# Larger packets for a decoder trunk's cache copies and near rows

## The reference

```
h = rms_norm(x, norm_g)
proj = einsum('btd,de->bte', h, w_in)
... convolution group -> ya, pooling group -> yb
kk = concatenate([k_buf, k], axis=1)
vv = concatenate([v_buf, v], axis=1)
o = dilated_attention(q, kk, vv, k_buf.shape[1])     # dilations 1, 4, 16, keys by stride
yc = o.reshape(B, T, C_ATT) * silu(c_gate)
new_k, new_v = kk[:, -2048:], vv[:, -2048:]
y = einsum('bte,ed->btd', concatenate([ya, yb, yc]), w_out);  return x + y, ...
```

## Time and profile before

| what | us |
|---|---|
| median of 3 runs | 404.59 |
| lowest, highest | 402.63, 405.35 |
| the profiled execution | 401.57 |
| its span, first to last instruction | 399.7 |

### The profile page before, as it was taken

The page is one execution under the profiler, slowest core; times in us unless marked ns, Lnnn a source line. Parts: engine busy times, 40 slices in busy tenths (PEclk is TensorE's granted clock), DMA queues, the critical chain, the costliest instruction groups (busy, mean ns, idle before and its releaser), DMA issues.

```text
span 399.7 us, 4745 instructions
## 1 busy us (share of the span) xinstructions
PE 347.5 (87%) x1550; PEld 273.4 (68%) x1550; DVE 232.6 (58%) x530; ACT 100.2 (25%) x237; POOL 58.8 (15%) x110
## 2 busy tenths in 40 slices
PE   3898799999889859899948999999979877989990
PEld 2686578887667636588827888888757654758870
DVE  2604669859977976620103489978984997541010
ACT  4200012542523123500111011453352222320011
POOL 4006830000600002044000420000600011000000
PEclk9999969999889899999986999999979988989997
DMA  8999999999999999999999999999999999999983
GB/s 293 412 419 412 418 418 417 418 407 411 417 419 408 418 392 406 396 418 418 416 398 387 414 418 416 417 411 420 418 419 417 414 357 361 372 374 372 396 347 118
DMA packets 44329, 157.73 MB, mean 395 GB/s; under 512 B 6988, under 2 KB 20116, under 8 KB 44306
## 3 DMA queue, kind: packets, MB, share of 16 engines
q0 software_dynamic: 14624, 88.25, 54.6%
q10 hardware_dynamic: 14420, 41.52, 26.3%
q1 hardware_dynamic: 15262, 27.67, 18.7%
HBM read 140.23 MB, written 104.46 MB: 612 GB/s over the span
## 4 chain that ended last, share of the span: by engine, by line
PE 43%; DVE 13%; SPq 12%; ACTq 11%; DMA 10%; issue 5%; ACT 4%; DVEq 0%
PE pj L693 23%; SPq L479 11%; DMA kg<-in_cache_k_win 10%; PE pj L836 8%; ACTq L459 4%; DVE yc L1296 3%; ACTq L465 3%; PE psc L765 3%; PE ptr L611 3%; DVE ssc L1240 2%; ACTq L463 2%; PE ps L813 1%; ACTq L874 1%; DVE spsum_pad L1266 1%; DVE tok L1234 1%
## 5 line engine op out<-in xcount | busy, mean ns | idle before, releaser
L693 PE MATMUL pj<-hT,wt 128*128 128x264 f32 x800 | 197.9, 407 | 6.3 <-DVE hT L1151 4.5
L693 PEld LDWEIGHTS pj<-hT,wt 128*128 128x128 f32 x800 | 159.0, 202 | 39.7 <-issue 11.6
L1296 DVE SCALAR_TENSOR_TENSOR yc<-u_ext,par,yc 128x256 f32<-128x256 f32 x180 | 77.2, 481 | 3.8 <-DVE u_smp L1180 1.0
L836 PE MATMUL pj<-mix,wt 128*128 128x264 f32 x256 | 61.2, 395 | 0.0
L836 PEld LDWEIGHTS pj<-mix,wt 128*128 128x128 f32 x256 | 49.1, 194 | 8.5
L600 POOL DMA_DIRECT2D out<-in_cache_v_win x48 | 26.2, 554 | 142.3 <-issue 142.3
L1366 DVE TENSOR_TENSOR xT<-xT,pj 128x264 f32<-128x264 f32 x16 | 6.9, 430 | 55.9 <-PE pj L836 55.9
L600 POOL DMA_DIRECT2D out<-in_cache_k_win x48 | 26.5, 561 | 83.6 <-issue 83.6
L954 ACT ACTIVATE ex<-pj 128x264 f32<-128x264 f32 x22 | 8.6, 391 | 78.3 <-PE pj L693 45.2
L1178 DVE SCALAR_TENSOR_TENSOR u_ext<-ex,pj 128x256 f32<-128x256 f32 x6 | 2.5, 422 | 30.5 <-ACT ex L954 30.5
L1234 DVE TENSOR_TENSOR tok<-kg,qb 128x1536 f32<-128x1536 f32 x10 | 17.6, 1758 | 3.4 <-DMA kg<-in_cache_k_win 3.0
(11 more groups left out here) (187 smaller groups left out, 339.6 us busy)
## 6 DMA issues: line engine op xcount, KB each, us to landing
wt<-in_w_tiles ACTq DMA_DIRECT2D x62, 512.0 KB, 33.2
out<-in_cache_k_win POOLq DMA_DIRECT2D x24, 1080.0 KB, 44.4
out<-in_cache_v_win POOLq DMA_DIRECT2D x24, 1080.0 KB, 81.1
out<-in_cache_k_win POOLq DMA_DIRECT2D x8, 1200.0 KB, 72.7
out<-in_cache_v_win POOLq DMA_DIRECT2D x8, 1200.0 KB, 87.9
out<-in_cache_k_win POOLq DMA_DIRECT2D x16, 432.0 KB, 65.1
out<-in_cache_v_win POOLq DMA_DIRECT2D x16, 432.0 KB, 86.2
kg<-in_cache_k_win SPq DMA_DIRECT2D x32, 144.0 KB, 36.0
```

Of the source, the lines that this page charges most:

```text
L693: last = nc.tensor.matmul(pj[n % RING][:, 0:T], wt[:, g % WRING, k, :], hT[:, k, :], start=(k == 0), stop=(k == KD - 1))
L836: last = nc.tensor.matmul(pj[n % RING][:, 0:T], wt[:, g % WRING, k, :], mix[:, k, :], start=(k == 0), stop=(k == KD - 1))
L1296: last = V.scalar_tensor_tensor(out=yc[:, t, 0:SEQ], in0=x_w, scalar=par[:, ROW_CW + w * CT + t:ROW_CW + w * CT + t + 1], in1=yc[:, t, 0:S ...
```

## The change

Only the lengths of the pieces change; the transfers, their order and their bytes stay. `NEAR_BYTES` goes from 4 rows (6144 B) to 8 (12288 B), so that a partition's near rows are one packet in gathers and stores. `DEEP_BYTES`, for layer 1's copies, goes from a third of 15 rows (7680 B) to half of them (11520 B). Layer 0's copies, cut into pieces of 5 rows (7680 B), are cut into 5 pieces for each of 16 parts: 9 rows (13824 B) for the copy of 720 rows and 10 rows (15360 B) for that of 800.

```diff
-COPY_BYTES = PIECE_ROWS * C_ATT * 4
-DEEP_BYTES = (DEEP_STEP - 1) * C_ATT * 4 // 3
+PIECES = 5
+DEEP_BYTES = (DEEP_STEP - 1) * C_ATT * 4 // 2
 BLOCK_BYTES = (FAR_STEP - 1) * C_ATT * 4
...
-NEAR_BYTES = 4 * C_ATT * 4
+NEAR_BYTES = GATHER[0][2] * C_ATT * 4
...
                     else:
-                        dst, src = (t.rearrange("(c e r) h d -> c e (r h d)", c=16, r=PIECE_ROWS) for t in (out[l, s, a:b], cache[l, s, a + 1:b + 1]))
-                        size = COPY_BYTES
+                        dst, src = (t.rearrange("(c e r) h d -> c e (r h d)", c=16, e=PIECES) for t in (out[l, s, a:b], cache[l, s, a + 1:b + 1]))
+                        size = (b - a) // (16 * PIECES) * C_ATT * 4
```

## The result

The changed kernel takes 450.62 us (median of 4 runs, 448.08 to 459.79), the kernel before it, timed beside it, 404.97 us (402.63 to 409.78): a ratio of 1.1113, with a 95% interval of 1.1068 to 1.1158. The run of 459.79 was a slow one and is left out of the ratio. Slower, as forecast, but by 46 us where 26 to 31 were forecast, and outside the range of 412 to 446.

A forecast was written before the change was run, and what follows sets the result against it. It took the full DMA engines, served in turns by packet, to bound the kernel through late gathers and ACT's held issue. Span 399.7 + 34 - 1 = 433, 434.6 us per execution, lowered to 431; range 412 to 446.

The forecast's parts named there:

- F: ACT's issue before layer 1, held by its full queue: +26 us, so PE starts layer 1 at 237 us.
- A: Landing of layer 0's first gathered keys: +6.3 us, so DVE starts at 94.7 us.
- D: Landing of layer 1's gathered keys: +34.7 us, at 305.6; DVE waits 8 us and everything after is late by 34.
- Turns: At the DMA engines: one packet of each busy queue in turn, whatever the sizes; a turn lasts 0.417 us.
- B: Landing of layer 0's first gathered values: +12.3 us, at 161.1 us; PE is +10.2 us from here.
- The size of a turn: q0's mean turn grows 67 ns in layer 1's copies, 112 in layer 0's: turns of 0.48 and 0.53 us.
- a gain of 4864 x 9.5 ns/16 = 2.9 us: Over all transfers: 4864 fewer packets, each saving a fixed 9.5 ns, take 2.9 us off DMA time.
- The weights have slack too: Weight tiles for PE: claimed to have time to spare and add no wait; no size given.
- E: Landing of layer 1's gathered values: +25 us, at 358, before PE's 369; no new wait; last copy near 350.
- The end: Compute after layer 1's keys are read, 128.2 us with idle DMA: about 1 us back, span 433 us.
- weights bind as well: Rival: during layer 0's copies a weight tile takes 4.8 us where PE needs about 4; 447 us, chance 10%.

The follow-up runs named there:

- small_copies: The kernel before with copies in packets of 4608 B (4800 B in transfers of 800 rows), near rows still 6144 B: 410.61 us, ratio 1.0255.
- after_no_value_stores: The changed kernel without layer 0's stores of gathered value rows, which ACT issues into q10: 435.46 us, ratio 1.0881 to the kernel before.
- after_no_key_stores: The changed kernel without layer 0's stores of gathered key rows, which SP issues into q1: 442.87 us, ratio 1.1061 to the kernel before.
- no_copies: The kernel before without all of POOL's cache copies and the waits for them: 378.8 us, ratio 0.9466.
- half_copies: The kernel before with copies of 7680 B set to 3840 B, near rows and far blocks unchanged: 402.8 us, ratio 0.9974.

## Why the prediction was wrong in size

The order of the forecast held (larger packets of q0, longer turns, late gathers, a later end). Two steps failed: the lengthening of a turn was put too low, +67 ns where it was +97, and the hold of ACT at its issues was counted only at F, although ACT's tile issues also delay the compute before A and add 16.6 us between F and D. By its own steps:

- **Turns** ("an engine serves them in turns, one packet of each, whatever the sizes"): right. Counts were equal at every size that was run, and small_copies shows the opposite sign at A, B and D. The Trainium skill's rule ("DMA: Bandwidth & Descriptors", section "Queues, rings and completion order"), a round-robin at packet granularity, agrees with 594, 596 and 596. Equal counts show that no queue gets ahead, not that the engines change queue after every single packet.
- **The size of a turn** ("The others' turn of 0.417 us becomes 0.48 and 0.53"): this term was mis-sized. From the counts of 100 to 200 us, a turn was 1600/3896 = 0.411 us and is 1600/3147 = 0.508: +97 ns where +67 were forecast. q0's own part went from 0.584 x 0.411 = 0.240 to 0.632 x 0.508 = 0.321, +81 for 1904 B more, where the fit's 0.0380 ns per byte gives +72; most of the rest is q10's, whose packets took 0.131 us instead of 0.122. In 200 to 300 us a turn is 0.555. The step behind it, a fit of 26.3 B/ns and 9.5 ns a packet taken as fixed, fell: all engines together moved 396 GB/s where it had been 411. That this is the memory, where q0 counts double, is argued above and not shown. For the same reason "a gain of 4864 x 9.5 ns/16 = 2.9 us" was not there, at least in the copies (277.03 against 276.42 us alone).
- **A**: right within 1.6 us (96.3 for 94.7), by luck in good part. q0 had 2536/16 = 158 turns by then, where the forecast counted 180 less some 8 for its 2 us of dry time; POOL waited 33.3 us for its state load, where it had waited 26.7, and in 40 to 46 us q0 had 71 packets beside 355 of q10. So q0 fell dry as assumed, but for longer, and that made up for turns that were longer than forecast. DVE's wait was 2.0 us instead of 9, because DVE itself was 9 us late, with no gather in its way: ACT's issue of five tiles took 13.23 us from 23.11 on (7.66 before), and three more in 62 to 74 us took 2.4 to 2.9 each instead of 0.3. In the chain of the first 100 us ACT's issuing of tiles has 22.7%.
- **B**: 170.0 for 161.1. From A to B it took 142.5 turns before, (5282 - 3002)/16, and (4818 - 2536)/16 = 142.6 after, so no turn was saved by the merged near rows; each took 0.517 instead of 0.425 us, 13 us in all where +6 were forecast.
- **F**: the mechanism was right (ACT's issue, not the data, decides), the size again the turn's: 248.7 for 237.
- **D**: "DVE would come at 271.5 + 26 = 297.5 and waits 8 us" (the compute keeps its pace behind F, and the keys decide) is the step that failed by mechanism, and "The weights have slack too" hid it. The weight tiles did land in time, some 20 us ahead of use by a rough reading of landings against readers, and I had looked at landings alone. But ACT, which issues them between its own computations, is held at each issue while its queue is behind. ACT's tile issues in layer 1 before the change,

```profile
268.87 0.34 ACTq L874 DMA_DIRECT2D wt<-in_w_tiles  x1
...
277.71 0.33 ACTq L874 DMA_DIRECT2D wt<-in_w_tiles  x1
...
282.16 0.33 ACTq L874 DMA_DIRECT2D wt<-in_w_tiles  x1
```

and after it (the row at 303.85 is one of the computations between the issues, for which PE waits):

```profile
288.60 3.37 ACTq L874 DMA_DIRECT2D wt<-in_w_tiles  x1
...
292.88 4.45 ACTq L874 DMA_DIRECT2D wt<-in_w_tiles  x1
...
298.25 4.28 ACTq L874 DMA_DIRECT2D wt<-in_w_tiles  x1
...
303.85 0.48 ACT L900 ACTIVATE r_qk<-ps,cst 128x264 f32<-128x264 f32 x1
...
307.62 5.17 ACTq L874 DMA_DIRECT2D wt<-in_w_tiles  x1
```

From 0.33 us an issue to 3.4 to 5.2. What ACT computes for PE comes late by that, as PE's timeline shows,

```profile
304.48 1.22 PE L703 MATMUL ps<-sqg,cst 128*128 128x264 f32 x2 [6.18 <-ACT r_qk L900]
```

and so 16.6 us are added between F, 37.8 us late, and the reader at D, 54.4 us late; the landing of the keys, 44 us late, would explain less. ACT's waits ahead of its line 900 (r_qk), put down to issue, are 24.0 us over the whole changed kernel and 1.6 over the kernel before. The chains that ended last say the same of the whole: ACTq, ACT's issuing, has 11% of the kernel before,

```profile
PE 43%; DVE 13%; SPq 12%; ACTq 11%; DMA 10%; issue 5%; ACT 4%; DVEq 0%
```

and 25% of the changed one:

```profile
PE 42%; ACTq 25%; DVE 16%; ACT 9%; issue 5%; DMA 2%; another core or an unknown queue 1%; DVEq 0%
```

That the stretch from F to D is long only where these issues are slow is shown by after_no_value_stores (59.1 us) beside after_no_key_stores (74.9). The 73.5 us of small_copies are the exception, by its wait for the store of the states.
- **E** ("its last copy lands near 350, after which the others have the engines", and "No new wait"): the first is wrong, the second came true narrowly. At D q0 had (10784 - 9023)/16 = 110 turns left, at 0.59 us each, and its last copy landed at 389.7. In 315 to 370 us the turns were still equal,

```profile
q0 software_dynamic: 1490, 13.50, 61.7%
q10 hardware_dynamic: 1492, 5.26, 25.0%
q1 hardware_dynamic: 1490, 2.81, 14.3%
```

and only in 370 to 389 us did the others pass it:

```profile
q1 hardware_dynamic: 1688, 2.41, 39.8%
q10 hardware_dynamic: 726, 1.97, 26.4%
q0 software_dynamic: 269, 1.33, 17.2%
```

The values landed at 388.6 for a forecast of 358, and PE came to them at 391.1, so 2.5 us were to spare and not 11. The stretch added 1.5 us to the readers' delay (54.4 at D, 55.9 at E).
- **The end** ("What follows is compute, 128.2 us from 271.5 to 399.7"): a misreading of the kernel before. Its last computation on ACT started at 390.11, and the span then lasted 9.6 us more, until ACT's last value stores had landed at 399.2. In the changed kernel it starts at 444.50, 54.4 us later, which is the delay at D to the tenth, and the span ends 4.2 us behind it. The lines are of the chains that ended last, before and after:

```profile
390.11 0.59 ACT hT L1087
```

```profile
444.50 0.59 ACT hT L1087
```

So 5 us came back because the DMA was free at the end, where 1 was forecast.
- The rival *weights bind as well*, 447 us, was closest in time, and close in place: it had the tile's landing as the reason, and it was the tile's issue. That its 447 came near 450.62 is therefore luck.

In sum, in us: +8 at A, +21 at B, +38 at F, +54 at D, +49 at the end.

Why none of the other sizes was faster than 7680 B: without the copies the kernel needs 377 us (no_copies), and the memory traffic of 140.23 + 104.46 = 244.7 MB, at the 65.3 MB per 100 us of the copies alone, would take 375 us, an estimate. The kernel before spans 399.7 and serves both nearly at once. Sizes between 7680 and 11520 B were not run.

## What to carry to other kernels

Where queues share the DMA engines, the packet size of a background queue acts as its priority (here from 4608 to 15360 B): a larger one delays everything that is waited for, and a smaller one delays the background. Judge a size by the turn (16 engines' time over the packet count of a saturated queue), do not take the rate as fixed, and try counting the bytes of a memory-to-memory copy twice, which fitted the stretches of 100 to 200 us here. Look also at what ends last, the compute or the transfers, before and after: a delay of the compute counts in full only where it ends last. And where an engine both computes and issues transfers, read its issue times, not only the landings: here the issuer, ACT, was late while the tiles still landed some 20 us ahead of their use.

## What the hardware showed that I had not expected

- Copies alone ran at 327 GB/s, some 650 GB/s read and written, with packets of 7680 B and with packets of up to 15360 B alike.
- An engine that issues transfers is held while its queue is behind: a tile's issue by ACT went from 0.33 us to as much as 5.17, and the stretch from F to D grew by 17 us with it.
- By the counts, adjoining pieces of 3840 B left as packets of 7680 B (14624 packets of q0 in half_copies, the number of before).
- Near rows in one packet cost 0.7% alone and gain 2% beside large copies. Why they cost alone stays open: the transfers, not the compute, end late there.
